# Scores of cached keys in a decoder step: key pages spread over all partitions by feature quarter, four column strips, half a sample at a time

## The reference, cut to what matters

```python
def sample_attention(q, k_new, v_new, lam, k_cache, v_cache, page_table, layer):
    k_past = k_cache[layer, page_table].reshape(b, -1, N_HEADS, 2, HEAD_DIM)   # 8 heads, 2 x 64 features
    v_past = v_cache[layer, page_table].reshape(b, -1, N_HEADS, V_DIM)
    s_past = jnp.einsum('bqhcd,bkhcd->bhcqk', q, k_past, preferred_element_type=jnp.float32)
    s_new = jnp.einsum('bqhcd,bkhcd->bhcqk', q, k_new, preferred_element_type=jnp.float32)
    s_new = jnp.where(jnp.tril(jnp.ones((t, t), dtype=bool)), s_new, NEG)
    s = jnp.concatenate([s_past, s_new], axis=-1) * scale
    p = diff_probs(s, lam).astype(v_new.dtype)      # softmax of component 0 minus lam times that of component 1
    return (jnp.einsum('bhqk,bkhe->bqhe', p[..., :n_past], v_past)
            + jnp.einsum('bhqk,bkhe->bqhe', p[..., n_past:], v_new))
```

## Time and profile before

| | |
|---|---|
| median of 3 runs | 2107.42 us (2106.15 to 2110.71) |
| the profiled execution: time, span | 2115.86 us, 2114.1 us |
| PE, DVE, ACT, POOL busy | 97%, 53%, 29%, 23% of the span |
| mean granted TensorE clock | 0.988 |
| PE idle in the waits view, in all | about 55 us |
| HBM read and written | 162.73 MB, 24.62 MB |
| instructions | 35690 |

### The profile page before, as it was taken

The page is one execution under the profiler, slowest core; times in us unless marked ns, Lnnn a source line. Parts: engine busy times, 40 slices in busy tenths (PEclk is TensorE's granted clock), DMA queues, the critical chain, the costliest instruction groups (busy, mean ns, idle before and its releaser), DMA issues.

```text
span 2114.1 us, 35690 instructions
## 1 busy us (share of the span) xinstructions
PE 2055.5 (97%) x14393; PEld 1863.8 (88%) x14393; DVE 1117.7 (53%) x1471; ACT 608.3 (29%) x1200; POOL 496.7 (23%) x373
## 2 busy tenths in 40 slices
PE   9999999998887989999999999999999999999999
PEld 8888888886775757999999988999999999999997
DVE  6766666664542333266553443554555555555556
ACT  5444445443311111224112422311221122122120
POOL 5333232421111111242331111311221121122120
PEclk9999999999998989999999999999999999999999
DMA  5222212114388786311224320211110111012112
GB/s 150 57 62 57 61 46 56 37 52 122 120 282 286 252 297 210 97 40 50 87 80 124 118 97 11 70 31 41 50 60 12 61 50 41 31 50 61 31 40 96
DMA packets 190791, 189.18 MB, mean 89 GB/s; under 512 B 21536, under 2 KB 164396, under 8 KB 190516
## 3 DMA queue, kind: packets, MB, share of 16 engines
q1 hardware_dynamic: 175660, 176.53, 26.3%
q10 hardware_dynamic: 14992, 10.62, 1.6%
HBM read 162.73 MB, written 24.62 MB: 89 GB/s over the span
## 4 chain that ended last, share of the span: by engine, by line
PE 93%; DMA 3%; SPq 2%; DVE 1%; issue 1%; POOL 0%; ACT 0%; POOLq 0%; DVEq 0%
PE PS L1488 39%; PE PS L2255 13%; PE PS L1016 6%; PE PS L2010 4%; PE PS L282 4%; PE PS L284 4%; PE PS L283 4%; PE PS L338 3%; PE PS L362 3%; DMA v_pg<-in_cache_v_dram 2%; PE PS L1098 2%; PE PS L351 2%; PE PS L1131 1%; PE PS L1509 1%; PE PS L1521 1%
## 5 line engine op out<-in xcount | busy, mean ns | idle before, releaser
L1475 POOL TENSOR_TENSOR fw_lo<-fw_raw,fw_hi 128x1024 fp32r<-128x1024 f32 x86 | 214.6, 2495 | 823.5 <-ACT fw_hi L1471 823.5
L1488 PE MATMUL PS<-m_hi,fw_hi 128*128 128x384 f32 (+1 forms) x1032 | 228.3, 329 | 0.0
L1488 PE MATMUL PS<-m_lo,fw_hi 128*128 128x384 f32 (+1 forms) x1032 | 227.5, 328 | 0.0
L1488 PE MATMUL PS<-m_hi,fw_lo 128*128 128x384 f32 (+1 forms) x1032 | 227.5, 328 | 0.0
L2383 DVE TENSOR_TENSOR x<-x,PS 128x512 f32<-128x512 f32 x198 | 136.2, 688 | 143.6 <-PE PS L2255 143.3
L1488 PEld LDWEIGHTS PS<-m_hi,fw_lo 128*128 128x128 f32 x1032 | 176.3, 188 | 0.0
L1488 PEld LDWEIGHTS PS<-m_lo,fw_hi 128*128 128x128 f32 x1032 | 176.3, 188 | 0.0
L1488 PEld LDWEIGHTS PS<-m_hi,fw_hi 128*128 128x128 f32 x1032 | 176.0, 188 | 0.4 <-POOL fw_lo L1475 0.2
L282 PE MATMUL PS<-w_hi,act_hi 128*128 128x384 f32 (+1 forms) x456 | 164.7, 361 | 0.0
L284 PE MATMUL PS<-w_hi,act_lo 128*128 128x384 f32 (+1 forms) x456 | 153.6, 337 | 0.0
L283 PE MATMUL PS<-w_lo,act_hi 128*128 128x384 f32 (+1 forms) x456 | 153.1, 336 | 0.0
(11 more groups left out here) (316 smaller groups left out, 4235.0 us busy)
## 6 DMA issues: line engine op xcount, KB each, us to landing
k_ring<-in_cache_k_dram SPq DMA_DIRECT2D x64, 512.0 KB, 5.7
v_pg<-in_cache_v_dram SPq DMA_DIRECT2D x56, 512.0 KB, 6.3
fw_raw<-in_w_up_dram SPq DMA_DIRECT2D x44, 512.0 KB, 3.9
fw_raw<-in_w_in_dram SPq DMA_DIRECT2D x24, 512.0 KB, 4.7
wd_raw<-in_w_down_dram SPq DMA_DIRECT2D x22, 512.0 KB, 4.4
w_raw<-in_w_in_dram SPq DMA_DIRECT2D x21, 512.0 KB, 5.2
out_dram<-raw SPq DMA_DIRECT2D x16, 512.0 KB, 3.7
sa_ring<-ga_scratch SPq DMA_DIRECT2D x8, 544.0 KB, 3.6
```

What stands on the lines that cost most here:

```text
L1475: e.tensor_tensor(fw_lo[slot][:, 0:kts, :], fw_raw[:, 0:kts, :], fw_hi[slot][:, 0:kts, :].bitcast(F32), ALU.subtract).then_inc(fw_tail, 1)
L1488: ins = e.matmul(PS[:, 3 * slot + c, 0:cw], w[slot][:, kt, :], x[:, kt, c0:c0 + cw], start=first and kt == 0, stop=last and kt == KT - 1)
```

## The change

Each key page is loaded by four DMAs instead of one. DMA i takes a quarter of the features (256 of 1024) of all 128 keys and puts them on the 32 partitions of quadrant i: partition k of the quadrant gets keys k, 32+k, 64+k and 96+k, 1 KB each. After the same turn by DVE a partition holds one feature of each of four quarters, and all 128 partitions together 32 features of each. So a matmul takes 128 rows and 32 columns (a strip of the array), with 512 columns of keys: 16 for the pages and 8 for the new keys. Rows of scores are now in another order, so `pick` and `coef` change with them.

The queries of all samples are laid out once by ACT, in 32 copies in the last head (`act_block_queries`: `q_s` and, for the new keys, `k_s`), and GpSimd makes a sample's `q_blk` (two buffers now) with one multiplication by a mask of its own rows. The trip of the queries through DRAM is gone.

The score of a sample is split into two halves of four pages, each with its own increment of `sc_full`, so SP can refill the first group of the ring earlier. In sample 0 a chunk stands between the halves. SP's order in a sample becomes: four key pages after the first half, two key pages after the second, then value, key, value, key, and the other values. Before phase 2 SP loads the four first key pages ahead of the stores of the last head, then three more, then two value pages. DVE turns four pages in the last head, at s = 5 to 8.

```diff
+                if group and not proj:
+                    act_block_queries(e)
...
+        def act_block_queries(e):
+            e.wait_ge(b7_free, b_use(NH - 1, False, ("k", 2)) + 1)
+            for src, dst in ((qT_s, q_s), (kT_s, k_s)):
+                for g in range(HG):
+                    for x in range(XB):
+                        ins = e.activation(dst[g * QB:(g + 1) * QB, :, :].rearrange("p (a x) t -> p x a t", a=2)[:, x, :, :],
+                                           src[x * QB:(x + 1) * QB, 2 * g:2 * g + 2, :], ACT.Copy)
+            ins.then_inc(qs_ready, 1)
...
-                if not proj and 1 <= s <= KEYS_TURNED_EARLY:
-                    dve_turn_keys(e, s - 1)
+                if not proj and s > QT - KEYS_TURNED_EARLY:
+                    dve_turn_keys(e, s - QT + KEYS_TURNED_EARLY - 1)
...
-        KEYS_TURNED_EARLY = KEYS_EARLY // 2 * 2
+        KEYS_TURNED_EARLY = 4
...
-                    for i in range(4):
-                        part = slice(i * QB, (i + 1) * QB)
-                        for g in range(HG):
-                            c = (2 * g + r) * VD + x * QB
-                            ins = e.matmul(PS[g * QB:(g + 1) * QB, B_S + i, 0:2 * P], queries(g, r, x, part),
-                                           pages[part, :, :, c:c + QB], start=r == 0 and x == 0, stop=r == 1 and x == XB - 1)
+                    c = (2 * x + r) * QB
+                    keys = k_ring[:, s:s + KEY_GROUP, :].rearrange("p j (a n) -> p (j a) n", a=HG)[:, :, c:c + QB]
+                    ins = e.matmul(PS[x * QB:(x + 1) * QB, B_S + half, :], q_blk[b % 2][:, x, r, :], keys,
+                                   start=r == 0, stop=r == 1)
...
-                pe_scores_of_sample(e, b)
-                fill[0]()
+                pe_new_scores(e, b)
+                pe_page_scores(e, b, 0)
+                if b == 0:
+                    fill[0]()
+                pe_page_scores(e, b, 1)
+                if b:
+                    fill[0]()
...
-            sp_load_page(e, g, k_ring[:, g % RK, :], k_ld[g % RK // 2], cache_k)
+            page = e.value_load(pgt[0:1, g:g + 1], min_val=0, max_val=NPHYS - 1)
+            keys = cache_k[0, bass.ds(page, 1)].rearrange("a (c k) h d -> (a k) c (h d)", k=QB)
+            for i in range(HG):
+                e.dma_start(k_ring[i * QB:(i + 1) * QB, g % RK, :].rearrange("p (c n) -> p c n", c=HG),
+                            keys[:, :, i * 2 * VD:(i + 1) * 2 * VD]).then_inc(k_ld[g % RK // 2], 16)
...
-            e.wait_ge(b7_free, b_use(NH - 1, False, ("k", 2)) + 1)
-            for b in range(NB):
-                e.dma_start(q_dram[:, b, :, :], qT_s[:, :, b * NS:(b + 1) * NS]).then_inc(q_st, 16)
-            e.wait_ge(q_st, 16 * NB)
-            for b in range(2):
-                sp_load_queries(e, b)
...
+                e.wait_ge(sc_full, 2 * b + 1)
+                keys(0, KEY_GROUP)
                 sp_chunk(e, fill[0])
+                e.wait_ge(sc_full, 2 * b + 2)
...
+                keys(KEY_GROUP, KEY_GROUP + 2)
+                sp_chunk(e, fill[1])
+                for k in range(2):
+                    values(k, k + 1)
+                    keys(KEY_GROUP + 2 + k, KEY_GROUP + 3 + k)
+                values(2, KEY_GROUP)
+                sp_chunk(e, fill[2])
+                values(KEY_GROUP, NPG)
```

More of the change, by code:

```diff
@@ L945, in build_step @@
         window = r("window", [P, 2 * NSAMP])
-        q_blk = r("q_blk", [P, HG, XB, 2 * QB])
+        q_s = r("q_s", [P, 2 * XB, NSAMP])
+        q_blk = [r(f"q_blk{i}", [P, XB, 2, QB]) for i in range(2)]
         late_pg = [r(f"v_pg{j}", [P, NH * VD]) for j in range(2, 5)]
@@ L949, in build_step @@
         es = r("es", [P, PASTK + PAGE])
-        pts = [r(f"pts{i}", [P, NPG if i < 1 else 1, NH * NS]) for i in range(2)]
         os_sb = [r(f"os_sb{i}", [P, 2 * VD]) for i in range(2)]
         ga_row = r("ga_row", [P, TOK])
-        q_c = [r(f"q_c{i}", [P, XB, NH * NS]) for i in range(2)]
+        pts = [r("pts0", [P, NPG, NH * NS])]
+        r = Region(both_at, pgt_at)
+        k_s = r("k_s", [P, 2 * XB, NSAMP])
+        pts.append(r("pts1", [P, 1, NH * NS]))
         smax = r("smax", [P, 2, 4])
@@ L966, in build_step @@
         vn_ld = sem("vn_ld")
-        q_st = sem("q_st")
-        qc_ld = [sem(f"qc_ld{i}") for i in range(2)]
+        qs_ready = sem("qs_ready")
         qb_ready = sem("qb_ready")
@@ L1064, in phase1_over, with pe_new_scores @@
                 e.wait_ge(kv_st[i], NH // 2 * 64 + 1)
-        def key_groups(b):
-            first, second = 2 * b % 3, (2 * b + 1) % 3
-            return min(first, second), max(first, second), first > second
-        def page_block(b, j):
-            half, i = divmod(j, KEY_GROUP)
-            return (1 - half if key_groups(b)[2] else half) * KEY_GROUP + i
-        def queries(g, r, x, part):
-            return q_blk[part, g, x, r * QB:(r + 1) * QB]
-        def pe_scores_of_sample(e, b):
-            lo, hi, _ = key_groups(b)
-            pages = k_ring[:, :, :].rearrange("p (g j) n -> p g j n", j=KEY_GROUP)[:, lo:hi + 1:hi - lo, :, :]
+        def pe_new_scores(e, b):
             e.wait_ge(qb_ready, b + 1)
@@ L1262, in pool_phase2 @@
                 fill = chunks_of(b)
-                if b + 1 < NB:
+                if b and b + 1 < NB:
                     pool_queries(e, b + 1)
@@ L1283, in sp_load_last_values @@
             sp_load_page(e, (NB - 1) * NPG + j, k_ring[:, END_SLOT + j, :], k_ld[(END_SLOT + j) // 2], cache_v)
-        def sp_load_queries(e, b):
-            for i in range(4):
-                e.dma_start(q_c[b % 2][i * QB:(i + 1) * QB, :, :],
-                            q_dram[:, b, :, :].rearrange("(x d) h q -> d x (h q)", d=QB)).then_inc(qc_ld[b % 2], 16)
         def sp_load_new_values(e):
@@ L1323, in sp_phase2, with keys, values @@
                 fill = chunks_of(b)
-                e.wait_ge(sc_full, b + 1)
-                for g in range(RK + b * NPG, RK + b * NPG + KEY_GROUP):
-                    if g < NB * NPG:
+                def keys(first, last):
+                    for g in range(RK + b * NPG + first, min(RK + b * NPG + last, NB * NPG)):
                         sp_load_keys(e, g)
-                sp_chunk(e, fill[0])
-                sp_chunk(e, fill[1])
-                if b + 2 < NB:
-                    e.wait_ge(qb_ready, b + 1)
-                    sp_load_queries(e, b + 2)
-                for g in range(RK + b * NPG + KEY_GROUP, RK + (b + 1) * NPG):
-                    if g < NB * NPG:
-                        sp_load_keys(e, g)
+                def values(first, last):
+                    for g in range(RV + b * NPG + first, min(RV + b * NPG + last, (NB - 1) * NPG)):
+                        sp_load_values(e, g)
+                e.wait_ge(sc_full, 2 * b + 1)
+                keys(0, KEY_GROUP)
+                sp_chunk(e, fill[0])
+                e.wait_ge(sc_full, 2 * b + 2)
                 if b >= NB - 2:
```

100 lines of the change are left out of this document (50 added, 50 removed).

## The result

The changed kernel takes 2142.81 us (median of 4 runs, 2140.84 to 2145.54), the kernel before, on the same chip, 2108.23 (median of 4 runs, 2106.15 to 2110.71): a ratio of 1.015, 95% interval 1.0134 to 1.0166. The forecast was 2086.0 with 2066 to 2114 around it; the change makes the kernel slower, and by more than the range allowed.

A forecast was written before the change was run, and what follows sets the result against it. It took PE's waits, mostly for value pages late behind SP's queue, as the bound. Terms -12 + 2 + 7.7 - 10.5 - 6.7 - 2.4 = -21.9 us took 2107.42 to about 2086, range 2066 to 2114.

The forecast's parts named there:

- the middle sample: Samples 1 to 5 of phase 2: 35.0 us each instead of 37.1, so five samples gain 10.5 us.
- lands ... I take 3.8: Middle sample: the third value page, which PE needs last, lands 3.8 us after its DMA starts at 25.8.
- six key pages, 15.6: Middle sample, SP's queue: issuing six key pages after the first half of the scores takes 15.6 us, 2.60 a page.
- slow clock after the waits 0.5: End of a middle sample: PE's lowered clock after its waits costs 0.5 us.
- Scores: PE's scores in each sample: 4.1 us instead of 6.5, 2.4 us gained where PE is what is late.
- Sample 0: Phase 2, from key page 7 to sample 1: 50 us instead of 42.3, 7.7 us lost.
- Sample 6: Phase 2, with fewer pages to load: PE sets it, 27.3 us against 34.0, 6.7 us gained.
- 12 us gained: Last head: PE's 10.5 us wait behind DVE goes, and 1.5 us of low clock with it.
- Nothing: GpSimd's mask product, shorter DVE chain, queries' DRAM trip: covered, no effect; if two chunks did not cover, 1 to 2 us cost.
- 2 us lost: Last head: ACT's 32 copies at 0.2 us each delay PE by 2 us, 1.4 to 5 at the bounds.
- Rival (a): Samples 0 to 5: SP's queue is the bound, 0.58 us a quarter, 29 us come back, 2114.5 us; chance 0.20.
- Rival (c): DMA engines are the bound: 1 KB pieces move slower, landing 2.5 us later in six samples, +15, 2100 us; chance 0.14.

The follow-up runs named there:

- experiment 2: Changed kernel with ACT's 32 copies spread over six steps of the last head instead of all in one: 2134.37 us, ratio 1.0105.
- experiment 8: Kernel of experiment 2 with quarters 2 and 3 of each key page issued from ACT's queue in phase 2: 2127.96 us, ratio 1.0066.
- 10: Kernel of experiment 2 with the four quarters of a key page issued in the order 0, 2, 1, 3: 2127.75 us, ratio 1.0091.
- 3: Changed kernel with each of the four key DMAs a page over all 128 partitions, 1 KB pieces, keys mislaid: 2135.93 us, ratio 1.0099.
- 9: Kernel of experiment 8 with every key DMA over all 128 partitions in 1 KB pieces, keys mislaid: 2102.69 us, ratio 0.9962.
- experiment 1: Changed kernel, keys mislaid, each key page by four DMAs in 4 KB pieces: 2141.0 us; two in 1 KB pieces: 2103.4; one in 4 KB rows: 2086.7.
- 5: Kernel before with only the four key-page turns of the last head moved to steps 5 to 8: 2110.13 us, ratio 0.9985.
- 4: Kernel before with only each key page loaded by four DMAs of 32 keys: 2183.73 us, ratio 1.0327.

## Why the prediction was wrong

The runs leave two limits, side by side: the issues ahead of the value pages, and the rate at which full DMA engines work on narrow key DMAs. Issue after the first score and landing of the third value page in sample 1:

| key DMAs a page | issued by SP alone | by SP and ACT |
|---|---|---|
| four of 32 partitions | 27.5 + 6.85 us (2, ratio 1.0105) | 23.9 + 10.15 us (8, 1.0066) |
| the same in another order | 28.4 + 4.52 us (10, 1.0091) | not tried |
| four of 128 partitions | 28.9 + 4.48 us (3, 1.0099; copies not spread) | 24.2 + 6.31 us (9, 0.9962) |
| one of 128 partitions | 20.5 + 5.95 us (0.9879; copies not spread) | not tried |

In the ratios, taken at 2110 us, the second queue alone is worth 8 us (1.0105 to 1.0066), and both limits off are worth 30 (1.0105 to 0.9962). Width adds 22 us with the second queue and 11 without it (1.015 to 1.0099, copies in one row in both): either limit hides part of what the other costs. The second queue shortens SP's part, but by the chain of experiment 8 ACT's own order then sets the issue, so 24 us is not the least that two queues can reach.

**The failed step** is the middle sample, 35.0 us forecast, 42.9 in sample 1, 41.4 in the mean of samples 1 to 5. Three of its terms were too small, by some 2 us each, and one was right:

- "lands ... I take 3.8": measured 6.32 in sample 1 and 5.9 in the mean of five, 2.1 us too little. The step argued that SP now issues 200 GB/s where 291 had been moved at a share of 0.84. That reads a rate as if it were a property of the engines. It is one of the DMAs they work on: with quarters to 32 partitions the engines were full at 231 to 266 GB/s. No row of before had such DMAs in number, and nothing spoke against the old 6.3. It stood only in a rival, with piece size as the reason, which experiment 1 excludes.
- "six key pages, 15.6": 17.3, and the third value page is issued at 29.4 in sample 1 and 28.0 in the mean, not 25.8. The undisturbed page is right (2.60 forecast). Single issues of up to 2.44 us among the 0.317 ones make the most of the rest, the value pages' price about 0.5 us. What holds the long issues was not separated from the full engines.
- "slow clock after the waits 0.5": the chain of sample 1 gives 0.9 us for the value products (1.91 against 1.0) and 0.9 for the last chunk (5.25 against 4.4 with its half microsecond); in the mean of five samples it is 2.1 us.
- Scores: forecast 4.1; 0.36 + 2 x 1.76 = 3.9 measured. **Right**, and sample 7, where nothing else is late, gained 2.6 us, 2.4 forecast. (The "25 ns each" of the old records is a slip: 6.5 us and 320 records give 20. The forecast does not use it.)

PE's timeline for the third term, the first and later matmuls of the chunk behind the wait:

```profile
653.68 1.05 PE L1132 MATMUL PS<-v_pg,pts 128*16 128x256 f32 x8 [2.35 <-DMA v_pg<-in_cache_v_dram]
...
656.48 0.47 PE L1031 MATMUL PS<-act_hi,fw_hi 128*128 128x320 f32 x1
656.75 0.47 PE L1031 MATMUL PS<-act_lo,fw_hi 128*128 128x320 f32 x1
...
659.36 0.31 PE L1031 MATMUL PS<-act_hi,fw_hi 128*128 128x320 f32 x1
659.50 0.31 PE L1031 MATMUL PS<-act_lo,fw_hi 128*128 128x320 f32 x1
```

PE waited for values for 6.4, 3.7 and 2.4 us, 12.4 of the 14.6 us before 653.7. The granted clock fell in the first of these waits and is 0.50, the level of 1.2 GHz, from 642 to 658; matmuls start 0.27 us apart there and 0.15 after 659, at 2.4 GHz. A late value page costs its wait and then 2 us more of slow work.

**Sample 0** had the same terms with 13 pages rather than 8: +14.6, not +7.7. Its third value page was issued 41.9 us behind key page 7 (40.1 forecast) and took 7.79 to land (3.8 forecast), its largest miss.

**Sample 6** was to be set by PE. Its value pages still land in 6.58 us behind four key pages of quarters, so it stayed at 35.2 us: an application of the first failed step.

**The last head.** "12 us gained" was 12.5 (experiment 2), right as a number and in part by luck: with the turns' place alone (5) a wait of 4.2 us takes the place of the old one, and it hangs on the queries' trip through DRAM, which the prediction put under "Nothing". "2 us lost" to the copies was 6.4. A copy of 32 partitions by 128 elements takes 0.31 us, and they start 0.32 apart: above the upper bound of 0.29. Fewer partitions bought nothing, and the overlap of neighbours, that other pairs show, was absent. The forecast let 0.2 stand against a row that said 0.27.

**The sum.** From the forecast's -21.9 us to the span's +29.6 it is 51.5 us. Of these 11 are the issue of the third value page in samples 1 to 5, 11 its landing, 10 the slow work behind the waits; 7 are sample 0, 8 sample 6, 4 the last head, and 1 sample 7 with the new wait at line 1518 (rounded, so that they add to 52). No one of these terms alone leaves the range.

**The rivals.** Rival (a) named one place and the sign. Its price, 0.58 us a quarter, is not what a quarter's DMA takes (0.317), and its 29 us are not what the queue cost: the third value page is issued 13 us later than forecast in samples 0 to 5 together. Rival (c) named the second limit, by the wrong mechanism; its 15 us were right in size (14.6 in samples 0 to 5). Together they give 2130, with the 4.4 us more for the copies 2134, against 2142.8 measured, and even that is partly luck, as (a) is 16 us too dear while the low clock and sample 6 are in neither. The range was made by taking rivals one at a time, when both hang on the same DMAs and so come together.

The prediction set aside the Trainium skill, DMA: Bandwidth & Descriptors, section Measured, with its advice to batch to 1 MiB or more, as the estimate of 9.2 us a key page from its fit was far off. A key page measured 2.6 to 2.9 us on the queue, so the setting aside of the size was right; the direction of the advice was not refuted by that, and experiments 1 and 4 bear it out (one DMA a page instead of four: 54 and 70 us).

**What stays open.** Why DMAs into 32 partitions keep the engines busy for fewer bytes, and why their order seems to change that; what makes single issues long; what a second queue gives where it does not stand ahead of ACT's own work. A version of the change with few wide DMAs, which lays the keys as the scores need them, was not tried: the one with a single DMA a page shows only that 2087 us are what such a layout could reach.

## What to carry to other kernels

When a load is split, count its DMAs on the issuing queue ahead of the transfer that ends the stage, and do not assume that its bytes move at the old rate: look at how many partitions each DMA writes, and keep the old landing time as a bound. Two costs that come from the same DMAs belong in one case, summed, and not in two rivals. A second queue has an order of its own: look at what stands behind the issues that are put there. Where a chain is cut, ask what was covered by the wait that goes: the last head gave 12.5 us with the whole change and 3 with the turns' move alone.

## What the runs showed of the hardware

- DMA engines that are fully busy moved 272 and 300 GB/s with key quarters to 32 partitions among the values, 386 and 400 GB/s with quarters to 128, at the same number of DMAs, 1 KB pieces and queues, in the same place of the sample (experiments 8 and 9). With the quarters issued in the order 0, 2, 1, 3 value pages landed in 4.2 to 5.3 us, not 5.3 to 7.1 (third page of samples 1 to 5, experiments 10 and 2).
- Pieces of 4 KB in place of 1 KB, both to 32 partitions, moved the time by 0.1% (experiment 1).
- With narrow quarters a second issuing queue put the third value page 3.6 us ahead, and it landed 3.3 us slower (sample 1, experiments 2 and 8).
- A quarter's DMA of 128 KB, in 128 pieces of 1 KB, issues in 0.317 us (changed kernel), a page of 512 KB in 128 pieces of 4 KB in 0.337 (before), half a page in 256 pieces of 1 KB in 0.543 (experiment 1, two DMAs): the bytes do not set it, and the number of DMAs does not alone.
- ACT copies 32 by 128 elements from SBUF to SBUF in 0.31 us, more than the 0.27 us of a 128 by 128 evacuation from PSUM, with no overlap between neighbours.
